# A gated MLP on one core: the sums of the up-projection's weight blocks are stored in DRAM in the first span of tokens and loaded again in the second

## The reference

```
h = rmsnorm(x, norm_ffn_pre)                       # 2048 x 1024
up = causal_depthwise_conv(h @ w_up, conv_w, conv_b)   # w_up: 1024 x 5632, conv over 3 tokens
gate, val = up[..., :2816], up[..., 2816:]
f = (silu(gate) * val) @ w_down
x = x + rmsnorm(f, norm_ffn_post)
```

## Time and profile before

| | |
|---|---|
| time, median of 3 runs | 2390.17 us (2389.98 to 2394.18) |
| the profiled execution's own time | 2389.26 us |
| its span in the trace | 2387.5 us (1.8 us lie around it) |
| PE busy over the span | 2339.1 us, 98% |
| DVE busy | 1777.1 us, 74% |
| POOL busy | 1014.5 us, 42% |
| up phase, on PE | from 1100 to about 1960 us |

### The profile page before, as it was taken

One profiled execution on the slowest core, in us unless ns is written; L12 is line 12 of the kernel. 1 busy time (PEld: TensorE's weight loads), 2 busy tenths in 40 slices (PEclk: granted clock), 3 DMA queues, 4 the chain that ended last, 5 costly groups with the idle time before them and its releaser, 6 DMA issues. The chain is left out here.

```text
span 2387.5 us, 36839 instructions
## 1 busy us (share of the span) xinstructions
PE 2339.1 (98%) x11791; PEld 1959.4 (82%) x11791; DVE 1777.1 (74%) x2105; ACT 1212.2 (51%) x2107; POOL 1014.5 (42%) x769
## 2 busy tenths in 40 slices
PE   9999999999999999998999999999999999999998
PEld 7887887888888888887888888778888878888887
DVE  5434214999999987888999988999999983354566
ACT  5311113889898975556444444544444443342353
POOL 0000002876667753555454555255554521040642
PEclk9999999999999999999999999999999999999999
DMA  6412438333333325678233332433232335455585
GB/s 196 141 49 80 140 124 212 73 107 87 83 88 87 94 73 182 214 218 263 92 116 105 105 105 92 172 115 106 92 110 88 111 107 172 157 180 184 203 296 185
DMA packets 260686, 322.65 MB, mean 135 GB/s; under 512 B 12948, under 2 KB 181836, under 8 KB 255564
## 3 DMA queue, kind: packets, MB, share of 16 engines
q1 hardware_dynamic: 258252, 312.62, 42.2%
q0 software_dynamic: 2304, 8.39, 0.9%
HBM read 211.38 MB, written 109.58 MB: 134 GB/s over the span
## 5 line engine op out<-in xcount | busy, mean ns | idle before, releaser
L847 POOL TENSOR_TENSOR weight<-beta,stick 128x512 f32<-128x512 f32 (+3 forms) x320 | 303.4, 958 | 523.9 <-DVE stick L890 486.1
L2337 DVE SCALAR_TENSOR_TENSOR x<-up_cols,taps,x 128x1024 f32<-128x1024 f32 x174 | 263.1, 1512 | 14.8 <-ACT x L2234 11.5
L890 DVE TENSOR_TENSOR_SCAN stick<-z_ps,stick,beta 128x512 f32<-128x512 f32 x192 | 245.4, 1278 | 14.6 <-ACT z_ps L785 13.4
L547 PE MATMUL out_ps<-hT,w_hi 128*128 128x512 f32 x768 | 238.4, 392 | 1.2 <-DVEq L474 1.2
L2324 DVE TENSOR_TENSOR wu_lo<-wu_sums,wu_hi 128x512 fp32r<-128x512 f32 x171 | 206.4, 1207 | 0.0
L784 ACT ACTIVATE beta<-z_ps 128x512 f32<-128x512 f32 (+3 forms) x320 | 171.3, 535 | 46.8 <-PE z_ps L922 40.8
L2221 ACT ACTIVATE wu_hi<-wu_sums 128x512 fp32r<-128x512 f32 x171 | 107.1, 627 | 152.4 <-PE gate_odd_ps L2505 78.9
L2505 PE MATMUL value_chain_ps<-wide,wu_hi 128*128 128x512 f32 x528 | 178.0, 391 | 3.2 <-DVE up_cols L2364 3.2
L939 PE MATMUL wT_ps<-ident,weight 128*128 128x128 f32 x1088 | 172.3, 274 | 1.3 <-POOL weight L847 1.3
L785 ACT ACTIVATE z_ps<-z_ps 128x512 f32<-128x512 f32 (+3 forms) x320 | 172.6, 539 | 0.0
L547 PEld LDWEIGHTS out_ps<-hT,w_hi 128*128 128x128 f32 x768 | 144.1, 188 | 33.4 <-issue 1.9
(11 more groups left out here) (297 smaller groups left out, 6226.2 us busy)
## 6 DMA issues: line engine op xcount, KB each, us to landing
f_scratch<-f_sum SPq DMA_DIRECT2D x88, 256.0 KB, 2.0
down_lo<-f_scratch SPq DMA_DIRECT2D x43, 512.0 KB, 3.4
wu_f<-in_w_up SPq DMA_DIRECT2D x42, 512.0 KB, 4.9
bridge<-in_w_up SPq DMA_DIRECT2D x42, 512.0 KB, 5.0
f_scratch<-x SPq DMA_DIRECT2D x66, 256.0 KB, 2.2
down_b<-in_w_down SPq DMA_DIRECT2D x64, 256.0 KB, 3.9
x_scratch<-x SPq DMA_DIRECT2D x56, 256.0 KB, 2.7
first_head<-qk_scratch SPq DMA_DIRECT2D x24, 512.0 KB, 10.2
```

Of the source, the lines that this page charges most:

```text
L547: m = pe.matmul(out_ps[half + j][:, :], w[slot][:, k, :], hT[h][:, k, j * BANK:(j + 1) * BANK], start=(k == 0 and t == 0), stop=(k == kc - ...
L847: pool.tensor_tensor(weight[v % weight_ring][:, 0:w], beta[v % stick_in][:, 0:w], stick[q % 2][:, at:at + w], ALU.mult).then_inc(weight_do ...
L890: dve.tensor_tensor_scan(stick[q % 2][:, at:at + w][:, ::-1], backwards, beta[u % stick_in][:, 0:w], start, ALU.mult, ALU.bypass).then_inc ...
L2337: dve.scalar_tensor_tensor(out=conv[h], in0=cols[:, h, 2 - back:2 - back + span], scalar=column(kind, h, e), in1=conv[h], op0=ALU.mult, op ...
```

## The change

In the first span SP stores the four sums of every unit but the last into a scratch in DRAM (`keep_sums`, four transfers of 256 KB), and POOL waits until the sums of unit u are stored before it makes those of unit u+1. In the second span POOL makes no sums; SP loads the four sums of unit u+1 with one transfer of 1 MB (`sums_again`), issued in unit u behind the load of the weights, and ACT waits for that transfer before it splits a sum. The sums of unit 23 are loaded at unit 21, ahead of the first `next_x`. The quarters are loaded as before. Four semaphores of a later phase become one.

```diff
-        late_x2_in = n.sems("late_x2_in", 4)
+        late_x2_in = n.sem("late_x2_in")
...
-                        dve.wait_ge(late_x2_in[t - 4], 16)
+                        dve.wait_ge(late_x2_in, 64)
...
+        sums_kept, sums_back = n.sem("wu_sums_kept"), n.sem("wu_sums_back")
...
                     if is_last(u):
                         start_loads(u)
+                    if part == 0 and not at_part_end(u, part):
+                        keep_sums(u, j)
                     if at_part_end(u, part):
+                        sp.wait_ge(sums_kept, 64 * (n_ff - 1))
+                        sums_again(u, block_of(part + 1, 1))
                         sp.wait_ge(even_out, stored(pair_sums, 32))
                         next_x(u, part, 0, 1)
...
                         load_w(block_of(part, j + 2), w_at(part, e))
+                    if part > 0 and not (past_part_end(u, part) or is_last(u)):
+                        sums_again(u, block_of(part, j + 1))
                     if not is_first(u):
                         store(u - 1, part, j, e, pair)
...
+                def keep_sums(u, j):
+                    for i in range(4):
+                        sp.wait_ge(wu_sum_done, 4 * u + (i + 1))
+                        sp.dma_start(s["w_sums"][j, i], sums[:, i, :, :].rearrange("p c n -> p (c n)")).then_inc(sums_kept, 16)
+
+                def sums_again(u, block):
+                    sp.wait_ge(wu_done, split_of(u, "s3"))
+                    sp.dma_start(sums[:, :, :, :].rearrange("p i c n -> p i (c n)"), s["w_sums"][block].rearrange("i p n -> p i n")).then_inc(sums_back, 16)
...
                     s1, s2, s4, s3 = (sums[:, i, :, :] for i in range(4))
+
+                    pool.wait_ge(sums_kept, 64 * u)
                     pool.wait_ge(w_in_[w_at(part, e)], loaded(part, pair))
...
                 def unit(u, part, j, e, pair):
-                    if at_part_end(u, part):
-                        pool.wait_ge(wu_sum_done, 4 * u + 4)
-                        pool.sem_inc(wu_sum_done, 4)
-                        left_sums(u + 2, part + 1, e, pair + 1)
-                    elif not (is_last(u) or past_part_end(u, part)):
+                    if part == 0 and not at_part_end(u, part):
                         left_sums(u + 1, part, 1 - e, pair + e)
...
                         act.wait_ge(w_in_[w_at(part, e)], loaded(part, pair))
+                    elif part > 0:
+                        act.wait_ge(sums_back, 16 * (u - n_ff))
                     else:
                         act.wait_ge(wu_sum_done, 4 * u + ("s1", "s2", "s4", "s3").index(operand) + 1)
...
+        "w_sums": scratch("w_sums_scratch", [a["n_ff2"] // 2, 4, P, a["kc"] // 2 * P], F32),
```

More of the change, by code:

```diff
@@ L1601, in load_late_x2 @@
                         sp.wait_ge(t_done, t4_made[n_k - 1])
-                    sp.dma_start(late_x2[i], s["x2"][token_tile(1, 4 + i)]).then_inc(late_x2_in[i], 16)
+                    sp.dma_start(late_x2[i], s["x2"][token_tile(1, 4 + i)]).then_inc(late_x2_in, 16)
                 def load_x2(half, t):
```

## The result

The changed kernel takes 2483.09 us (median of 4 runs, 2477.26 to 2484.68), the kernel before 2391.67 us beside it (2389.98 to 2394.18). The ratio is 1.0377, 95% interval 1.0365 to 1.0389: some 91 us slower, where 39.6 were forecast, and outside the range of 2405 to 2458.

The account below looks back on a forecast made before the run. PE was taken to bound the kernel, busy 98% of the span. Gaps 34.3, clock 6.8, change of span -3.5 and first span 2 sum to +39.6 on the profiled 2389.3: 2429 us, range 2405 to 2458.

Parts of the forecast that it names:

- The mechanism: Units 25 to 41: sums loaded behind the weights come late, so `gate_part` is late and PE stands ahead of s3t3.
- From T + 1.73 that makes T + 9.8: Second span, T being a unit's s1t1 start on PE: 8.05 us from first issue puts the loads' last byte at T + 9.8.
- added 0.6: Second span: 0.6 us from the loads' last byte to ACT's start on the sums, giving T + 10.4.
- T + 8.4 and T + 12.4: ACT's start on the sums: earliest if loaded as if alone, latest if as if issued only after the weights' bytes.
- 2.6 against 1.5: Units 25 to 41: PE gaps of 2.6 us in 8 even units and 1.5 in 9 odd ones, 34.3 us together.
- Half of the eight gaps of 2.6 us and none of the shorter: Clock drops behind the even units' gaps, at 1.7 us each: 6.8 us, bounds 0 and 29.
- every gap: Rival: every gap in units 25 to 41 drops the clock, 13 more drops of 1.7 us, 2451 us; chance 0.15.
- The change of span: Around unit 24: DVE comes some 6 us earlier, so the 1.78 us gap and its 1.7 of clock go, -3.5 us.
- `gate_part` would end at 1587 to 1588, just inside the fill: Unit 24: with DVE 6 us earlier, `gate_part` ends before the fill of idle matmuls does at 1588.31.
- the gap at 1531.91: End of the first span: PE's 2.00 us gap left unchanged, bounds -2 and +3 us.
- The first span: Extra stores delay POOL's sums and give DVE work before `gate_part`: 0 to 0.8 us per pair, 2 us taken, 8 at most.
- some 4 us late: Start of the first span: first unit's sums late by four issues and 2.0 us to land, counted inside the 2 us.

Follow-up runs that it names:

- the orders mended: Changed kernel with sums loaded ahead of weights, stores a unit earlier, unit 0's stores and second span's first load moved, against the kernel before: 2386.5 us, ratio 0.9979.

## Why the prediction was wrong

**The mechanism was right.** The gaps stand ahead of s3t3, in units 25 to 41 alone, put down to `gate_part`, with ScalarE idle for the sums. Moving the load alone takes them all away. Four sizes were off, all to the same side.

**When the sums arrive.** The step "From T + 1.73 that makes T + 9.8" is the one that failed first. It took the pair of loads in the earlier trace rows as its measure, 8.05 us from the first issue to the last byte. Here the loads' bytes ran from 1856.5 to about 1865.7, some 9.9 us from the first issue at 1855.81, at 255 GB/s and with a store of 256 KB among them, where the earlier trace rows had 314 GB/s. So the last byte came at T + 11.6, and ScalarE started right behind it, where the prediction added 0.6. Of the two ends that the prediction had, T + 8.4 and T + 12.4, the nearer was the one in which the sums behave as if issued only when the weights are through. Even units came out hardly worse than odd ones either (2.90 against 2.74 us, not 2.6 against 1.5): the sums are so late that GpSimd's work on f is nearly done (its last three sums took 1.28 us or so, where they were 1.62 to 1.76 before; the last began at 1889.10), and the low part takes 0.96 us, not 1.78. Gaps: 46.0 us against 34.3.

**The clock.** "Half of the eight gaps of 2.6 us and none of the shorter" gave 6.8 us; 15 of 17 gaps paid, 25.6 us. The four gaps of the earlier trace rows were too few to set a share, and the share was laid on gaps that had themselves come out too short: of the 16 gaps above 2.1 us, 15 dropped the clock (not the 2.75 of unit 39), and the one of 1.57 did not. Length alone does not settle it: the gaps of 3.35 and 2.28 at the start of the same execution, and one of 2.42 at 1594.33, had no drop behind them. Behind the 3.35:

```profile
1136.58:1144.00 7.42, 7.42 (x33) 6.16 (x34) 7.35 (x7) 4.75 (x6) 5.38 (x3) 1.00 0.01 2
```

The rival "every gap" had this term nearly right. The Trainium skill, "TensorE: Matmul & The Clock Gate", section "HAM oscillation — how this bites in real kernels", tells of a loop that pays a drop in each turn in which TensorE waits for a transfer, there for some 3 to 5 us; this trace agrees in 15 turns of 17, with waits of 2.17 to 2.93 us.

**The change of span.** Forecast -3.5, measured +6.7 (64.9 us between the two gaps in place of 58.2). The gain is there: with the orders mended the whole second span is 4.2 to 4.6 us shorter than before. What failed is "`gate_part` would end at 1587 to 1588, just inside the fill", by the same late landing: in unit 24 the gap is 4.60. The sums of unit 24 are late as well: ScalarE waits 9.30 us for them, and gaps of 0.47 and 2.42 us stand at the head of unit 24 where one of 0.65 stood. I had also left the gap at 1531.91 as it was, with +3 as its bound; the megabyte ahead of the tokens made `x_first` usable 8.96 us after its issue (1525.74 to 1534.70) in place of 5.68, and the gap 1.0 longer with a drop behind it.

**The first span.** Forecast +2, measured +11.7: 4.6 at the start (47.3 us from the phase's first matmul to unit 1's s3t3, in place of 42.8), 6.1 in the pairs behind it, and the 1.0 by which the gap at the end grew. A pair's gap is only 0.3 us, but with what a gap costs beyond its length (last section) eight pairs take 0.6 us each, and the first one 1.5. That is near the most that the prediction gave (0.8 a pair, 8 in all), where it took 2. At the start unit 0's stores stood in the queue behind the four of x's sums, issued from 1114.54 to 1121.28; GpSimd, which had no store to wait for, now waits 6.1 us for them, and ScalarE starts on unit 1's s1 at 1128.18, not 1120.94. Gaps of 3.35 and 2.28 follow where 0.91 and 1.43 stood; the next wait for stores, 10.0 us, ends at 1152.76, behind both. The prediction had put the start, "some 4 us late", inside the 2.

The terms as measured, 46.0 + 25.6 + 6.7 + 11.7 = 90.0 us, are within 3 us of what the up phase lost (953.5 against 860.8).

## What to carry to other kernels

Where a computed operand is turned into a loaded one, the load's place in its queue decides, and not only the sum of the bytes: ask for it as soon as its buffer is free, ahead of what is needed later. Here moving the load ahead gave back 82.6 us; a small first piece at the old place, 74.3. The same 42 MB of extra traffic (84 stores of 256 KB, 21 loads of 1 MB) cost 91 us in one order and gave 5 in another. A recurring wait of TensorE is to be priced with the clock drop that may stand behind it, here 1.7 us on top of 2.7 in 15 turns of 17. And work taken from engines that hide behind a busy TensorE is worth only what they hold up at the few places where TensorE does wait.

## What the runs showed of the hardware that I had not expected

Two loads of 1 MB in one queue, the first in 512 KB pieces of weights, the second in sums: the second lands 8.5 us after its issue behind the first, 5.7 us alone or ahead; from two queues at the same time 7.4, with the first slowed from 5.0 to 7.2. A load of 256 KB behind the same weights lands 5.3 us after its issue, while the stores of 256 KB land in 2.2 (medians).

A gap also costs more than its own length on the profile: with the load on the other queue a unit with a gap of 0.34 us takes 19.64 us (1862.70 to 1882.34) against 19.04 without one, at full clock. The rows there account for nearly all of the other 0.26 us:

```profile
1881.61 0.39 PE L2523 MATMUL gate_odd_ps<-wide,wu_lo 128*128 128x512 f32 x1
1882.34 0.47 PE L2523 MATMUL value_chain_ps<-wide,wu_hi 128*128 128x512 f32 x1 [0.34 <-DVE up_cols L2382]
1882.64 0.39 PE L2523 MATMUL value_chain_ps<-x_t_lo,wu_hi 128*128 128x512 f32 x1
```

Without a gap a matmul starts 0.227 us behind the one before it and overlaps its end. Ahead of the gap the whole 0.39 us of the last one counts, 0.16 more, and the second matmul behind the gap starts 0.30 behind the first, 0.07 more.
